# A decoder trunk on one core: shift mix and convolution read from PSUM, angles on ScalarE, all early weight rests on VectorE

## What is computed

```python
proj = h @ w_in
u_s5, p_ml, p_rw, p_mb = split_cols(proj, (GW, ML_COLS, RW_COLS, MB_COLS))

# RWKV-7 group: each column is mixed with its value one token earlier
prev = jnp.pad(p, ((0, 0), (1, 0), (0, 0)))[:, :-1]
p = p + (prev - p) * mu

# mLSTM group: a causal convolution over 4 tokens, per column, ahead of q and k
qk = silu(causal_dwconv(concatenate([q, k], -1), conv_w))
# ... and two gates per head: log_i, and the running sum of log_sigmoid(f)

# S5 group: a complex diagonal recurrence with decay exp(lr * step) and angle li * step
ab_re, ab_im = mag * cos(ang), mag * sin(ang)
```

## Time and profile before

| | |
|---|---|
| median of 3 runs | 572.63 us (571.75 to 575.11) |
| profiled execution | 574.52 us, its span 572.7 us |
| PE, DVE, ACT, POOL busy | 507.9, 400.5, 252.2, 227.0 us |
| share of PE in the chain that ended last | 71%, DVE 18%, ACT 4% |
| granted TensorE clock, mean | 0.95 |

### The profile page before, as it was taken

How to read it: one execution, slowest core, us unless ns; L and a number is a source line. 1 busy time by engine, 2 the same in 40 slices (tenths; PEclk the granted TensorE clock), 3 DMA queues, 4 the chain that set the end, 5 groups by cost and what they waited for, 6 DMA issues and landing times.

```text
span 572.7 us, 8465 instructions
## 1 busy us (share of the span) xinstructions
PE 507.9 (89%) x3490; PEld 457.5 (80%) x3490; DVE 400.5 (70%) x444; ACT 252.2 (44%) x386; POOL 227.0 (40%) x124
## 2 busy tenths in 40 slices
PE   0749999786899999998969989769999999999986
PEld 0739869676879988967859977569999999988875
DVE  5896577999766756579582442478999999983213
ACT  3555651232152224364684443644444544443333
POOL 2361339695335450133342203034343535344440
PEclk9969999797899999998988989969999999999999
DMA  8706257002103222442453432244654655456512
GB/s 347 297 25 251 82 176 258 1 0 75 43 31 129 93 74 74 148 148 74 148 202 129 148 110 74 74 148 146 212 196 150 216 192 178 156 212 219 162 60 74
DMA packets 12358, 79.22 MB, mean 138 GB/s; under 512 B 1440, under 2 KB 2080, under 8 KB 3488
## 3 DMA queue, kind: packets, MB, share of 16 engines
q1 hardware_dynamic: 12320, 78.68, 39.0%
HBM read 76.84 MB, written 1.84 MB: 137 GB/s over the span
## 4 chain that ended last, share of the span: by engine, by line
PE 71%; DVE 18%; ACT 4%; issue 3%; POOL 1%; DMA 1%; POOLq 0%; SPq 0%; DVEq 0%; ACTq 0%
PE bank L366 71%; DVE arena L1575 2%; POOL w_rest L347 1%; DMA ring<-weights 1%; ACT w_high L341 1%; DVE arena L1545 1%; DVE arena L1527 1%; DVE arena L1412 1%; DVE arena L1528 1%; DVE arena L1573 1%; DVE kx L1392 1%; DVE wm_rest L347 1%; DVE arena L1358 1%; DVE arena L1426 0%; DVE arena L1422 0%
## 5 line engine op out<-in xcount | busy, mean ns | idle before, releaser
L366 PE MATMUL bank<-h_high,w_high 128*128 128x256 f32 x480 | 131.5, 286 | 5.6 <-DVE h_rest L1882 3.3
L347 POOL TENSOR_TENSOR w_rest<-ring,w_high 128x1024 fp32r<-128x1024 f32 x30 | 73.1, 2439 | 141.9 <-ACT w_high L341 141.9
L366 PE MATMUL bank<-h_rest,w_high 128*128 128x256 f32 x448 | 127.8, 285 | 0.0
L366 PE MATMUL bank<-h_high,w_rest 128*128 128x256 f32 x416 | 118.7, 285 | 0.0
L341 ACT ACTIVATE w_high<-ring 128x1024 fp32r<-128x1024 f32 x68 | 71.4, 1058 | 71.9 <-PE bank L366 71.8
L366 PEld LDWEIGHTS bank<-h_high,w_high 128*128 128x128 f32 x480 | 90.7, 193 | 6.3 <-issue 6.2
L366 PEld LDWEIGHTS bank<-h_rest,w_high 128*128 128x128 f32 x448 | 86.5, 193 | 0.1
L366 PEld LDWEIGHTS bank<-h_high,w_rest 128*128 128x128 f32 x416 | 80.5, 193 | 0.0
L366 PE MATMUL bank<-arena 128*128 128x128 f32 (+7 forms) x496 | 64.6, 310 | 11.2 <-DVE arena L1585 5.8
L366 PEld LDWEIGHTS bank<-arena 128*128 128x128 f32 (+3 forms) x496 | 56.4, 191 | 18.2 <-issue 7.0
L347 DVE TENSOR_TENSOR w_rest<-ring,w_high 128x1024 fp32r<-128x1024 f32 x30 | 43.3, 1442 | 32.4 <-ACT w_high L341 32.4
(11 more groups left out here) (295 smaller groups left out, 1157.5 us busy)
## 6 DMA issues: line engine op xcount, KB each, us to landing
ring<-weights SPq DMA_DIRECT2D x50, 1024.0 KB, 5.0
third_slot<-weights SPq DMA_DIRECT2D x15, 1024.0 KB, 4.8
cst<-consts SPq DMA_DIRECT2D x1, 1664.0 KB, 12.1
gain<-gains SPq DMA_DIRECT2D x3, 512.0 KB, 5.9
par<-params SPq DMA_DIRECT2D x1, 1056.0 KB, 14.2
kx<-x_t SPq DMA_DIRECT2D x1, 1024.0 KB, 4.9
vx<-mem_t SPq DMA_DIRECT2D x1, 1024.0 KB, 8.9
xres<-x_rows SPq DMA_DIRECT2D x1, 1024.0 KB, 8.6
```

The source lines that it names most:

```text
L347: e.tensor_tensor(rest_, raw_half(i), high.bitcast(F32), ALU.subtract).then_inc(rest_done(i)[0], 1)
L366: return nc.tensor.matmul(out_, lhsT, rhs, start=start, stop=stop, skip_group_check=True)
```

## The change

Four edits, all ahead of the third level of the inverse, and the queues they move.

1. Shift mix. ACT no longer copies the projection to `rwP`; it writes (1 - mu) times it to `rwM`, two instructions (`shifted`), and VectorE adds mu times the column before, read from the PSUM bank, and frees the bank.
2. Convolution. ACT writes the newest tap (`conv_now`), VectorE adds the other three from PSUM (`conv_back`) and frees the bank: for ml_q ahead of the RWKV key work, for ml_k behind rests 16 and 17. The block between scan(0) and level_update(1) is gone.
3. The eight angle products and the rounding are on ACT, between its high parts; so are the four rel copies. The S5 coefficients (15 small instructions) run ahead of conv_back(0).
4. POOL makes none of the first 18 rests; VectorE makes all. POOL starts with the memory's sum and the S5 readout.

The gates are also turned: 16 products with 8 moving columns, a copy by ACT (`gate_cols`), and four transposes into `gate_rows`.

```diff
@@ TensorE, gates
-            for e in range(2):
+            for m in range(2):
                 for k in range(KD):
-                    last = mm(o[0:NH, e * T:(e + 1) * T], v3(prm("w_gate"), 8)[:, k, 4 * e:4 * e + 4],
-                              hT[:, k, :], k == 0, k == KD - 1)
+                    last = mm(o[:, 8 * m:8 * m + 8], hT[:, k, m * P:(m + 1) * P], v3(prm("w_gate"), 8)[:, k, :],
+                              m + k == 0, k == KD - 1)
...
             last.then_inc(full[3], 1)
+            o = pe_open(pe, "gate_rows", 2)
+            moved(pe, "gates")
+            for e in range(2):
+                for m in range(2):
+                    at_ = e * T + m * P
+                    last = nc.tensor.transpose(o[0:NH, at_:at_ + P], gate_cols[:, 8 * m + 4 * e:8 * m + 4 * e + 4],
+                                               const("ident"))
+            last.then_inc(full[2], 1)
@@ POOL
-            for i in range(1, H_MID, 2):
-                rest(pool, g, i)
-                if i == 3:
-                    pool.wait_ge(S["sq_m_ready"], 1)
-                    sum_tiles(pool, g, sq_m, "mem_summed")
...
+            pool.wait_ge(S["sq_m_ready"], 1)
+            sum_tiles(pool, g, sq_m, "mem_summed")
+            s5_readout()
@@ ACT
+            def shifted(name, n):
+                o = v3(wait_full(act, name)[:, :], T)
+                for c in range(2):
+                    i = 2 * n + c
+                    e = a.activation(rwM[:, i, :], o[:, c, :], ACT.Copy, scale=one_mu[:, i:i + 1])
+                e.then_inc(S["rw_cur"], 1)
+
+            def conv_now(name, n):
+                o = v3(wait_full(act, name)[:, :], T)
+                for c in range(2):
+                    i = 2 * n + c
+                    e = a.activation(cv[:, i, :], o[:, c, :], ACT.Copy, scale=prm("conv")[:, 4 * i + 3:4 * i + 4])
+                e.then_inc(S["ml_cur"], 1)
...
-            project("rw_wag", rwP[:, 0:2, 1:257])
+            act.wait_ge(S["half_ready"], 1)
+            shifted("rw_wag", 0)
             highs(6)
-            project("rw_k", rwP[:, 2:4, 1:257])
+            act.wait_ge(S["consts_in"], 16)
+            act.wait_ge(S["theta"], 3)
+            for i in range(8):
+                e = a.activation(sin[:, i, :], const("time"), ACT.Copy, scale=frac[:, i:i + 1])
+            e.then_inc(S["theta"], 1)
+            act.wait_ge(S["theta"], 4)
+            a.activation(cos, sin, ACT.Identity, bias=const("round")).then_inc(S["theta"], 1)
+            shifted("rw_k", 1)
             highs(8)
+            for h in range(NH):
+                o = wait_full(act, f"rel{h}")
+                a.activation(E[:, h, :], o[:, 0:384], ACT.Copy).then_inc(free_of(f"rel{h}"), 1)
             a.preload_act_table_set(SIN_TANH)
+            moved(act, "rw_wag")
+            a.activation(rwE[0:HD, 0, 0, :], rwM[0:HD, 0, :], ACT.Tanh).then_inc(S["rw_low"], 1)
+            a.activation(rwE[:, 0, 1, :], rwM[:, 1, :], ACT.Tanh, scale=0.5).then_inc(S["rw_exp"], 1)
             act.wait_ge(S["theta"], 6)
             a.activation(cos, sin, ACT.Abs).then_inc(S["sincos"], 1)
+            shifted("rw_r", 2)
+            highs(10)
             act.wait_ge(S["sincos"], 1)
             a.activation(cos, cos, ACT.Sin, bias=const("half_pi"), scale=-TAU).then_inc(S["sincos"], 1)
-            highs(9)
+            shifted("rw_v", 3)
+            highs(12)
             a.activation(sin, sin, ACT.Sin, scale=TAU).then_inc(S["sincos"], 1)
...
-            project("ml_q", raw[:, 0:2, 3:259])
+            conv_now("ml_q", 0)
             highs(16)
             inv_root("rw_kk", flat(rwE[:, 2]), 512, 1.0, "eps12").then_inc(S["rw_inv"], 1)
-            project("ml_k", raw[:, 2:4, 3:259])
+            conv_now("ml_k", 1)
             highs(18)
...
-            wait_full(act, "gates")
+            o = wait_full(act, "gates")
+            a.activation(gate_cols, o[:, 0:16], ACT.Copy).then_inc(free_of("gates"), 1)
@@ VectorE
-                    if split[0] % 2 == 0 or H_MID <= split[0] < H_LATE:
+                    if split[0] % 2 == 0 or split[0] < H_LATE:
                         rest(dve, v, split[0])
...
             def mix(n, name):
-                moved(dve, name)
-                v.tensor_tensor(rwM[:, 2 * n:2 * n + 2, :], rwP[:, 2 * n:2 * n + 2, 0:T], rwP[:, 2 * n:2 * n + 2, 1:T + 1],
-                                ALU.subtract).then_inc(S["rw_diff"], 1)
...
+                dve.wait_ge(S["rw_cur"], n + 1)
+                o = v3(wait_full(dve, name)[:, :], T)
+                for c in range(2):
+                    i = 2 * n + c
+                    last = v.scalar_tensor_tensor(rwM[:, i, 1:T], o[:, c, 0:T - 1], prm("mu")[:, i:i + 1],
+                                                  rwM[:, i, 1:T], ALU.mult, ALU.add)
+                last.then_inc(free_of(name), 1)
+
+            def conv_back(n, name):
+                cw = v3(prm("conv"), 4)
+                dve.wait_ge(S["ml_cur"], n + 1)
+                o = v3(wait_full(dve, name)[:, :], T)
+                for d in range(1, 4):
+                    if d > 1:
+                        dve.wait_ge(S["ml_conv"], 2 * n + d - 1)
+                    for c in range(2):
+                        i = 2 * n + c
+                        last = v.scalar_tensor_tensor(cv[:, i, d:T], o[:, c, 0:T - d], cw[:, i, 3 - d:4 - d],
+                                                      cv[:, i, d:T], ALU.mult, ALU.add)
+                    last.then_inc(S["ml_conv"] if d < 3 else free_of(name), 1)
```

More of the change, by code:

```diff
@@ L113, in trunk_kernel @@
         ring = sb("ring", EARLY_RING * SLOT)
-        small = sb("small", 160)
+        small = sb("small", 192)
         xres = v3(sb("xres", 2 * D)[:, :], D)
@@ L608, in _ @@
             o = v4(pe_open(pe, "rw_vt", 3)[:, :], 2, P)
-            pe.wait_ge(S["rw_mix"], 4)
+            moved(pe, "rw_v")
             for c in range(NC):
@@ L1120, in _ @@
             a.preload_act_table_set(EXP_TANH)
-            act.wait_ge(S["ml_conv"], 4)
+            moved(act, "ml_q")
+            moved(act, "ml_k")
             act.wait_ge(S["rel_stored"], 16)
@@ L1378, in _ @@
             v.tensor_scalar(neg_bglu, prm("b_glu"), -1.0, None, ALU.mult)
+            v.tensor_scalar(one_mu, prm("mu"), -1.0, 1.0, ALU.mult, ALU.add)
             v.tensor_scalar(one_ka, prm("k_a"), -0.5, 1.0, ALU.mult, ALU.add).then_inc(S["half_ready"], 1)
@@ L1435, in _ @@
             rests(8)
-            for h in range(NH):
-                o = wait_full(dve, f"rel{h}")
-                v.tensor_copy(E[:, h, :], o[:, 0:384]).then_inc(free_of(f"rel{h}"), 1)
+            dve.wait_ge(S["theta"], 5)
+            v.scalar_tensor_tensor(sin, cos, ROUND, sin, ALU.subtract, ALU.subtract).then_inc(S["theta"], 1)
             rests(9)
@@ L1445, in _ @@
             rests(12)
-            dve.wait_ge(S["rw_mix"], 4)
+            moved(dve, "rw_k")
             for j in range(2):
@@ L1471, in _ @@
             rests(14)
+            dve.wait_ge(S["sincos"], 3)
+            cos1, sin1, lr, li = cos[:, :, 1], sin[:, :, 1], prm("lam_re"), prm("lam_im")
+            v.tensor_tensor(s8b, mag, cos1, ALU.mult)
+            v.tensor_tensor(s8c, mag, sin1, ALU.mult)
+            v.tensor_tensor(den8, lr, lr, ALU.mult)
+            v.tensor_tensor(s8a, li, li, ALU.mult).then_inc(S["s5_co_step"], 1)
+            dve.wait_ge(S["s5_co_step"], 1)
+            v.tensor_tensor(den8, den8, s8a, ALU.add)
+            v.tensor_scalar(s8b, s8b, -1.0, None, ALU.add).then_inc(S["s5_co_step"], 1)
+            dve.wait_ge(S["s5_co_step"], 2)
+            v.reciprocal(den8, den8)
+            v.tensor_tensor(co_re, s8b, lr, ALU.mult)
+            v.tensor_tensor(s8a, s8c, li, ALU.mult)
+            v.tensor_tensor(co_im, s8c, lr, ALU.mult)
+            v.tensor_tensor(frn, s8b, li, ALU.mult).then_inc(S["s5_co_step"], 1)
+            dve.wait_ge(S["s5_co_step"], 3)
+            v.tensor_tensor(co_re, co_re, s8a, ALU.add)
+            v.tensor_tensor(co_im, co_im, frn, ALU.subtract).then_inc(S["s5_co_step"], 1)
+            dve.wait_ge(S["s5_co_step"], 4)
+            v.tensor_tensor(co_re, co_re, den8, ALU.mult)
+            v.tensor_tensor(co_im, co_im, den8, ALU.mult).then_inc(S["s5_co"], 1)
+            conv_back(0, "ml_q")
             moved(dve, "rw_a")
@@ L1496, in _ @@
             rests(18)
[L1498 to L1518 removed]
+            conv_back(1, "ml_k")
             rests(H_MID + 2)
@@ L1529, in scan @@
                 last.then_inc(S["scanned"], 1)
-            o = wait_full(dve, "gates")
+            o = wait_full(dve, "gate_rows")
             v.tensor_scalar(rows[0][0:NH, :], o[0:NH, T:2 * T], prm("f_bias", NH), None, ALU.add).then_inc(S["ml_gate"], 1)
-            v.tensor_scalar(rows[1][0:NH, :], o[0:NH, 0:T], prm("i_bias", NH), None, ALU.add).then_inc(free_of("gates"), 1)
+            v.tensor_scalar(rows[1][0:NH, :], o[0:NH, 0:T], prm("i_bias", NH), None, ALU.add).then_inc(free_of("gate_rows"), 1)
             dve.wait_ge(S["rstd_m"], 1)
```

(14 more changed lines are left out.)

93 lines of the change are left out of this document (23 added, 70 removed).

## The result

| | before | changed |
|---|---|---|
| median, run side by side (8 runs each) | 574.92 us (571.75 to 577.08) | 568.48 us (566.68 to 571.33) |
| profiled execution, its span | 574.52, 572.7 us | 568.71, 566.9 us |
| PE, DVE, ACT, POOL busy | 507.9, 400.5, 252.2, 227.0 us | 505.3, 381.4, 260.4, 198.9 us |
| granted TensorE clock, mean | 0.95 | 0.96 |

Ratio 0.9907 (95% interval 0.9885 to 0.9929): 5.3 us faster (4.1 to 6.6). The forecast was 11.0 us, or 1.9%: the sign is right, the size is half. 568.5 lies inside the range of 554.5 to 569, at its far end; the forecast was counted from a median of 572.6, and 0.9907 of that is 567.3.

What follows compares the result with a forecast made beforehand. TensorE, busy 89%, was taken as the bound, with waits and low clock before 145 us to win. The running sum, -9.4 at ml_k, -2.3 after bank 1's stop, -14.3 at mb_k, ended at -11.0: 561.6 us, range 554.5 to 569.

Steps and rivals of the forecast that it cites:

- Start and slot 2: Up to ml_k: first product 0.95 us earlier, 7.4 us wait and 1.95 of low clock gone; ml_k ends 9.4 earlier.
- rival B: Smaller gain, 567 us, chance 0.21: angle copies at 0.62 (1.9), late slot 2 (1), longer low clock behind new stops (2.5).
- The stop behind bank 1: Before s5_in(1): TensorE idles 8.4 us until VectorE frees ml_k's bank at 78.8; the gain shrinks to 2.3 us.
- The clock will be low after such an idle: 1.1 us: Behind the 8.4 us idle before s5_in(1): low TensorE clock costs 1.1 us.
- Level 1, mb_q: 3.8 us wait for POOL's mask goes, level_p(1) 6.1 earlier; 4.6 of low clock goes, mb_q ends 10.7 earlier.
- Convolution off the path: 17.7 us leave VectorE between scan(0) and level_update(1); s5_out(0) waits 3.3 us for POOL; mb_k ends 14.3 earlier.
- The rows: mLSTM rows: the chain through POOL's mask, rotation and scan(1) ends at 134.1, before 145.1: 11.0 us earlier; TensorE idles 6.1.
- is taken as equal to what stands there before: At the mLSTM rows: low clock after the 6.1 us idle equals that behind L1603's wait before, so no added cost.
- Rests on VectorE: Nine more rests on VectorE, 10.3 us, cost nothing beyond 2.3 behind ml_k and 0.5 at the start, already counted.
- A: Larger gain: scan(1) and the rows run unblocked by POOL, rows done at 128.6; -16.5, 556 us, chance 0.14.
- C: No change: as B, with the stop behind bank 1 12 us longer by contention; -1, 571 us, chance 0.06.
- D: Slower: VectorE's work behind ml_k takes contended times, taps 1.13 each, bank 1 free at 93.1; 575.9 us, chance 0.09.

Runs made afterwards that it cites:

- bank 5: The changed kernel with bu1 in PSUM bank 5 instead of bank 1, nothing else; ratio 0.9798 to the kernel before.

## Why the prediction was half right

- **Start and slot 2: right.** PE starts at 16.4 as said (16.65 found), the wait of 7.4 us is gone with its low clock, ml_k ends at 66.27 (66.1). ScalarE kept up: s5_u ends at 50.8. The reason, the angles and the subtractions leaving VectorE, was sufficient but not the only one: with the angles on VectorE and POOL silent the wait is gone as well. Angle copies at 0.41 and taps at 0.44 cost what the sum had. So rival B's first two terms did not come.
- **The stop behind bank 1: the wait right, the low clock behind it not.** 8.2 us forecast as 8.4, its end at 79.00 for 78.8. The step that failed is "The clock will be low after such an idle: 1.1 us". The clock was 0.50 until about 84.5, 5.5 us of work at half speed: 2.7 us. The sum took the work from the stop to ml_v, 2.05 us, at full speed and the low clock only behind it; that work took 3.62. With the clock at 1.00 (17 unused products) it took 2.33. So ml_v moves from 80.8 to 82.6, 0.2 of it from the later end of the stop, and A from 2.3 earlier to 0.5. The earlier trace rows had shown 3.9 to 9.3 us of low clock behind each stop of before. From the end of the stop to A the four kernels with it and the small gates take 15.7 to 17.1 us, where the sum had 14.6.
- **Level 1, mb_q: right in mechanism.** POOL's mask is no longer queued behind its rotation; the wait of 3.8 and the low clock after it went: 3.2 us up to level_p(1), forecast 3.8, then 3.7 more by the clock, forecast 4.6.
- **Convolution off the path: right.** VectorE is done with scan(0) at 109.5, POOL's rotation back takes 5.98 (5.16 forecast), TensorE waits 2.9 (3.3) for it; the wait of 5.8 goes.
- **The rows: clock wrong, and this is the larger part.** m_row comes 8.5 us earlier for 11.0: scan(0) ends 1.9 later than in the sum, mostly by the step above, the rotation back takes 0.8 more, POOL's mask and rotate(1) take 1.2 less than forecast, and scan(1) starts 1.0 behind POOL, since level_update(1) and a rest stand ahead of it on VectorE; the 10.4 us of scan(1) and rows are as forecast. TensorE idles 5.0 us in two pieces for the 6.1 of the sum. The low clock there "is taken as equal to what stands there before". That is the second step that failed. Before, g_col came without a wait and one stop of 2.53 us stood ahead of m_row; m_row itself took 2.08, near the 1.99 of full clock, and about 3 us at half speed followed. m_row of the kernel before, then the window:

```profile
145.18 2.08 PE L366 MATMUL bank<-arena,cst 4*128 4x256 f32 x8 [2.53 <-DVE arena L1603]
```

```profile
145.00:150.00 5.00, 4.83 (x21) 0.69 0.00 0
```

  Now two stops follow each other, 2.46 and 2.53 with 0.25 us of work between, and 0.50 holds from 136.7 to about 146: 9.4 us, 4.7 us lost for some 1.7 before. The difference is 3.0, and mb_v shows 2.9. The kernel with only these stops filled takes as long from m_row to mb_v as the one before.
- **Rests on VectorE: right in sign, too small.** I had them as costing nothing; they gain 3.2 us, by not contending.

So of rival B (567, -5.6) the time came true, but in part by luck: of its three terms only the third came, the low clock behind the new stops. B priced it at 2.5 us behind the stops of 3.3 and 8.4; what came is some 1.7 behind the one of 8.2 and up to 2.9 behind the rows' two stops, which B does not name. A is refuted by the stop of 2.53 ahead of m_row, C and D by the stop behind bank 1, 8.2 us long, and by the taps, which take 0.44, never 1.13.

The Trainium skill (SBUF — State Buffer, Who interferes with whom) says that a VectorE instruction with two SBUF inputs contends with a GpSimd instruction that reads SBUF, and one with at most one SBUF input, outside the modes that use both ports, does not. The rows here agree: the memory products take 3.23, 6.61 or 10.01 us by what POOL does beside them, the six taps 2.67 or 2.68 in every row shown. Either engine can be the one that stands: before, the memory products took 3.24 beside a POOL product that took 3.99, where the same one takes 0.62 in the changed kernel.

## To carry over

Price each new stop on TensorE at its length plus half of the low-clock stretch that the trace shows behind stops like it, over all the work that this stretch covers, and look for stops that now come in pairs. When a bank's freeing moves to an engine with a queue, ask who opens that bank next and give that user another one: here one digit was worth as much as the whole change. Moving work off an engine that contends with VectorE can gain more than that work costs VectorE: 3.2 us here for nine rests. And set a difference between two single profiles against how much the same stretch differs among all of them.

## Not expected of the hardware

- TensorE's clock fell while the engine was in unbroken work: with bank 5, towards the end of 16 products of 8 moving columns, from 1.00 to 0.51 in the 4 us from 70; with the same sums made by 16 products of 256 columns it stayed at 1.00. The Trainium skill (TensorE: Matmul & The Clock Gate, What's actually happening) says that a monitor sets the clock by how busy TensorE has been; the trace calls it busy there throughout (3.89 of the 4 us), so the profile's busy time alone would not have foretold this fall.
- The clock can read 1.00 through an idle stretch and fall only behind it: with the old gates and bank 1, 1.00 from 70 to 78 though TensorE stopped at 74.5, then 0.50 from 80 to 84.
- Products whose result nobody reads made the kernel faster: ten of them, in two stops of 2.5 us, by 0.8% (0.9825 for 0.9907).
